# A hybrid attention and mixture-of-experts layer: the input projection in 512-column products, and the first expert pass fixed to expert 0 with its weights loaded early

## The reference, cut to what matters

```
h    = rms_norm(x);  proj = h @ w_in                      # 512 x 1024 @ 1024 x 3072
mix  = concat(diff_attention(...), silu(gate) * norm(retention(...)))
x    = x + mix @ w_o
h2   = rms_norm(x);  logits = h2 @ w_router + b_router
top_val, top_idx = top_k(logits, 4);  gates = softmax(top_val)
for every expert e, over its tokens:
    u = h2[tokens] @ w_moe_in[e] + b;  a = swiglu_clamped(u)     # 1024 -> 2048 -> 1024
    y[tokens] += gates * (a @ w_moe_out[e] + b)
out  = rms_norm(x + y)
```

## Time and profile before

| | |
|---|---|
| median of 3 executions | 1530.5 us (1530.23 to 1533.79) |
| profiled execution, its own time | 1528.76 us |
| its span | 1527.1 us |
| mean granted TensorE clock | 0.977 of full |
| PE / DVE / ACT / POOL busy | 95% / 85% / 67% / 15% of the span |
| projection on PE | about 14 to 155.4 us |
| first product of pass 0 | 334.03 us |
| DMA | 462.93 MB, mean 303 GB/s |

### The profile page before, as it was taken

How to read it: one execution, slowest core, us unless ns; L and a number is a source line. 1 busy time by engine, 2 the same in 40 slices (tenths; PEclk the granted TensorE clock), 3 DMA queues, 4 the chain that set the end, 5 groups by cost and what they waited for, 6 DMA issues and landing times.

```text
span 1527.1 us, 23128 instructions
## 1 busy us (share of the span) xinstructions
PE 1452.4 (95%) x7349; PEld 1216.0 (80%) x7349; DVE 1291.6 (85%) x1149; ACT 1024.1 (67%) x914; POOL 236.2 (15%) x239
## 2 busy tenths in 40 slices
PE   7999679849999999999999999999999999999996
PEld 7999457737888888888888888888888888888884
DVE  5643664759999999999999999999999999999997
ACT  6222562327777777777777777777777777777774
POOL 0000401230111111111111111111111111111112
PEclk9999798959999999999999999999999999999999
DMA  9420100269999999999999999999999999999994
GB/s 320 141 84 28 42 1 21 52 235 343 359 368 360 372 364 361 373 372 375 370 370 369 370 376 362 377 366 360 364 373 377 368 370 367 371 366 375 366 369 166
DMA packets 137604, 462.93 MB, mean 303 GB/s; under 512 B 15620, under 2 KB 28200, under 8 KB 137512
## 3 DMA queue, kind: packets, MB, share of 16 engines
q1 hardware_dynamic: 124000, 442.55, 77.9%
q0 software_dynamic: 13248, 19.41, 5.2%
q10 hardware_dynamic: 328, 0.60, 0.1%
HBM read 459.57 MB, written 23.36 MB: 316 GB/s over the span
## 4 chain that ended last, share of the span: by engine, by line
PE 89%; DVE 4%; DMA 3%; ACT 2%; issue 1%; SPq 0%; POOLq 0%; POOL 0%; DVEq 0%; ACTq 0%
PE pair L921 23%; PE pair L923 23%; PE pair L929 23%; PE pair L634 3%; PE pair L639 3%; PE pair L635 3%; PE pair L935 2%; PE pair L947 2%; PE pair L897 2%; DMA ring<-in_w_moe_in 2%; PE pair L788 1%; PE pair L789 1%; PE pair L799 1%; DVE split L1707 1%; DMA expert_sums<-work,list_cur 1%
## 5 line engine op out<-in xcount | busy, mean ns | idle before, releaser
L1707 DVE TENSOR_TENSOR split<-ring,split 128x2048 fp32r<-128x2048 f32 x396 | 892.9, 2287 | 72.3 <-ACT split L1212 72.3
L1212 ACT CAST split<-ring 128x2048 fp32r<-128x2048 f32 x396 | 758.7, 1916 | 214.4 <-PE pair L929 194.6
L921 PE MATMUL pair<-split,operands 128*128 128x512 f32 x1584 | 631.1, 398 | 4.6 <-DVE operands L1712 4.6
L923 PE MATMUL pair<-split,operands 128*128 128x512 f32 x1584 | 618.9, 391 | 0.0
L929 PE MATMUL pair<-split,operands 128*128 128x512 f32 x1584 | 425.2, 390 | 0.0
L921 PEld LDWEIGHTS pair<-split,operands 128*128 128x128 f32 x1584 | 298.3, 188 | 64.0 <-DVE operands L1712 5.2
L929 PEld LDWEIGHTS pair<-split,operands 128*128 128x128 f32 x1584 | 297.9, 188 | 63.4
L923 PEld LDWEIGHTS pair<-split,operands 128*128 128x128 f32 x1584 | 298.4, 188 | 58.7
L1947 POOL DMA_INDIRECT expert_sums<-work,list_cur x32 | 60.9, 1904 | 462.3 <-PE pair L929 430.8
L1940 POOL DMA_INDIRECT work<-h_rows,token_next x35 | 72.4, 2069 | 183.8 <-DMA token_next<-slot_lists 168.2
L634 PE MATMUL pair<-split,operands 128*128 128x256 f32 x352 | 86.5, 283 | 1.0 <-DVE work L1388 1.0
(11 more groups left out here) (266 smaller groups left out, 1228.1 us busy)
## 6 DMA issues: line engine op xcount, KB each, us to landing
ring<-in_w_moe_in SPq DMA_DIRECT2D x264, 1024.0 KB, 9.3
ring<-in_w_moe_out SPq DMA_DIRECT2D x132, 1024.0 KB, 10.5
ring<-in_w_in SPq DMA_DIRECT2D x12, 1024.0 KB, 10.6
ring<-in_w_o SPq DMA_DIRECT2D x4, 1024.0 KB, 4.9
resid<-in_x SPq DMA_DIRECT2D x4, 512.0 KB, 5.4
expert_sums<-zero_rows SPq DMA_DIRECT2D x4, 512.0 KB, 8.7
work<-expert_sums SPq DMA_DIRECT2D x4, 512.0 KB, 5.2
out<-ring SPq DMA_DIRECT2D x4, 512.0 KB, 2.6
```

The source lines that it names most:

```text
L921: pe.matmul(dst[:, f, :], left_hi[:, k0 + k, :], hi[c.buffer][:, k, cols], start=(start and k == 0), stop=False)
L923: pe.matmul(dst[:, f, :], left_lo[:, k0 + k, :], hi[c.buffer][:, k, cols], start=False, stop=False)
L1212: act.copy(hi[c.buffer], raw[c.slot]).then_inc(hi_made, 1)
L1707: dve.tensor_tensor(lo[c.buffer], raw[c.slot], hi[c.buffer].bitcast(F32), ALU.subtract).then_inc(lo_made, 1)
```

## The change

It has four parts. The input projection now goes in 6 blocks of `BW` = 512 columns. A chunk is half a block's K tiles (4 of 8) by 512 columns, so it still has 1 MB, and there are still 12. Two chunks accumulate into one bank; blocks alternate between banks 0 to 3 and 4 to 7, and the transposes of q and k moved to banks 0 to 3. `w_out_lo` and `w_out_hi` stand ahead of the evictions in the last two chunks. In the output projection `mix_high` isn't cut in two around `bias_product` any more. In the routing `choose` makes `picked` with one comparison over 32 x 4 and one reduction; `read_places` also makes the 0/1 matrix of places of expert 0 for its tile; the search for the first expert with tokens is gone, expert 0 always gets pass 0 (and at least one pass, even if it has no tokens); the counts and the table of passes come after the gates. And SP loads the early chunks 0, 2, 3, 4 when the last high product of the output projection is done (`wo_high_done`), 1 and 5 after the whole of it; each chunk raises its own `raw_full`. POOL issues the scatter of tile 2 after clearing `x_rows`, and the load of the last norm's gain after the scatter of tile 3.

```diff
-NCHUNK = PROJ // CW
+BW = 512
+NBLOCK = PROJ // BW
+NCHUNK = 2 * NBLOCK
...
-            def first_chunk(e, n):
-                return up_chunk(e, n // QUARTERS, n % QUARTERS)
+            def first_load(n):
+                sp.dma_start(raw[n], up_chunk(0, n // QUARTERS, n % QUARTERS)).then_inc(raw_full[n], 16)
 
             for i in range(NT - 1):
                 sp.wait_ge(h2_ready, i + 1)
                 sp.dma_start(h2_dram[i * P:(i + 1) * P, :], h2_row[:, i, :]).then_inc(h2_stored, 16)
+            sp.wait_ge(wo_high_done, 1)
+            for n in (0, 2, 3, 4):
+                first_load(n)
             sp.wait_ge(wo_done, NT)
-            sp.wait_ge(b_out_split, 1)
-            sp.wait_ge(b_in_split, 2)
-            for n in range(RAW):
-                sp.dma_start(raw[n], first_chunk(0, n)).then_inc(early_loaded, 16)
-            load_pass_count(sp)
-            first = expert_of(0)
-            sp.wait_ge(early_loaded, 16 * RAW)
-            with sp.If(first < 1):
-                for n in range(RAW):
-                    sp.sem_inc(raw_full[n], 16)
-            with sp.Else():
-                for n in range(RAW):
-                    sp.dma_start(raw[n], first_chunk(first, n)).then_inc(raw_full[n], 16)
+            for n in (1, 5):
+                first_load(n)
             sp.wait_ge(pool_passed, 1)
             for k in range(RAW - QUARTERS, QUARTERS):
-                load(0, SECOND + k, up_chunk(first, 1, k))
+                load(0, SECOND + k, up_chunk(0, 1, k))
+            load_pass_count(sp)
             by_pass(sp, one_pass)
...
             for c in range(1, NCHUNK):
+                b, a, s = c // 2, c % 2, c % PARTS
                 pe.wait_ge(w_hi_made, c + 1)
                 for i in range(NT):
-                    u = c * NT + i
-                    pe.wait_ge(proj_by_act if u % 2 == 0 else proj_by_dve, (u - 4) // 2 + 1)
-                    dst, at_i, s = bank[u % 4][:, 0:CW], of_tile(i), c % PARTS
...
+                    if a == 0 and b >= 2:
+                        pe.wait_ge(proj_by_act if i % 2 == 0 else proj_by_dve, 2 * (b - 2) + i // 2 + 1)
+                    dst, at_i = bank[NT * (b % 2) + i], of_tile(i)
+                    for k in range(KH):
+                        pe.matmul(dst, hT_hi[:, KH * a + k, at_i], w_hi[s][:, k, :], start=(a == 0 and k == 0), stop=False)
+                        pe.matmul(dst, hT_lo[:, KH * a + k, at_i], w_hi[s][:, k, :], start=False, stop=False)
                     if i == 0:
                         pe.wait_ge(w_lo_made, c + 1)
-                    for k in range(KT):
-                        mm = pe.matmul(dst, hT_hi[:, k, at_i], w_lo[s][:, k, :], start=False, stop=(k == KT - 1))
-                    mm.then_inc(proj_ready, 1)
+                    for k in range(KH):
+                        mm = pe.matmul(dst, hT_hi[:, KH * a + k, at_i], w_lo[s][:, k, :],
+                                       start=False, stop=(a == 1 and k == KH - 1))
+                    if a == 1:
+                        mm.then_inc(proj_ready, 1)
+                    elif i == NT - 1:
+                        mm.then_inc(half_block_done, 1)
...
-                    mm = pe.transpose(bank[4 + g % 4][:, i * P:(i + 1) * P], proj[:, i, col:col + P], ident)
+                    mm = pe.transpose(bank[g % 4][:, i * P:(i + 1) * P], proj[:, i, col:col + P], ident)
...
+                    if i == NT - 1 and k == KT - 1:
+                        mm.then_inc(wo_high_done, 1)
...
-                mix_high(i, range(0, 4))
+                mix_high(i, range(KT))
                 bias_product(i - 2)
-                mix_high(i, range(4, KT))
                 router(i - 1)
                 mix_low(i)
             places(2)
+            def first_tokens(j):
+                pe.wait_ge(first_list_step, j + 1)
+                for a in range(2):
+                    mm = pe.matmul(bank[2][:, 256:257], first_slots[:, j, :], token_parts_bf[:, j, a:a + 1],
+                                   start=(j == 0 and a == 0), stop=(j == NT - 1 and a == 1))
+                if j == NT - 1:
+                    mm.then_inc(first_product, 1)
+
             router(3)
+            pe.wait_ge(tokens_named, 13)
+            for j in range(NT - 1):
+                first_tokens(j)
             places(3)
-            pe.wait_ge(tokens_named, 13)
-            pe.wait_ge(first_list_step, 1)
+            first_tokens(3)
             for j in range(NT):
-                mm = pe.matmul(bank[6][:, 64:66], first_slots[:, j, :], token_parts_bf[:, j, :],
+                mm = pe.matmul(bank[3][:, 64:64 + NE], ones_bf[:, :], picked_bf[:, j, :],
                                start=(j == 0), stop=(j == NT - 1))
-            mm.then_inc(first_product, 1)
+            mm.then_inc(place_ready, 1)
...
             for c in range(NCHUNK):
-                for i in range(1, NT, 2):
...
-                    if c >= NCHUNK - 2:
-                        w_out_lo(2 * (c - NCHUNK + 2) + i // 2)
-                if c in ROPE_CHUNKS:
-                    rotary(c)
+                if c == NCHUNK - 2:
+                    for q in range(3):
+                        w_out_lo(q)
+                if c == NCHUNK - 1:
+                    w_out_lo(3)
+                if c % 2:
+                    evict(c // 2, 1)
+                if c + 2 < NCHUNK:
+                    w_in_lo(c + 2)
+                if c % 2:
+                    evict(c // 2, 3)
+                    for n in (c - 1, c):
+                        if n in ROPE_CHUNKS:
+                            rotary(n)
...
                 dve.wait_ge(place_read, i + 1)
+                dve.tensor_scalar(first_slots[:, i, :], slot_number, within[:, i, 0:1], None, ALU.is_equal)\
+                    .then_inc(first_list_step, 1)
...
-                chain(dve.tensor_copy(top8_f, top8_i))
+                chain(dve.tensor_tensor(by_choice, expert_id.unsqueeze(2).to_broadcast([P, NE, TOPK]),
+                                        top8_i[:, 0:TOPK].unsqueeze(1).to_broadcast([P, NE, TOPK]), ALU.is_equal))
                 chain.settle()
-                for k in range(TOPK):
...
-                dve.tensor_copy(picked_bf[:, i, :], picked[:, i, :]).then_inc(picked_ready, 1)
+                with nc.allow_low_precision(reason="zeros and ones"):
+                    dve.tensor_reduce(picked_bf[:, i, :], by_choice, AX_X, ALU.add).then_inc(picked_ready, 1)
+                dve.wait_ge(picked_ready, i + 1)
...
-            h2_norm(NT - 1)
             read_places(NT - 2)
             place_entries(NT - 2)
...
-            dve.tensor_copy(expert_count, bank[7][:, 64:64 + NE]).then_inc(table_ready, 1)
...
-            dve.tensor_tensor(first_slots, slot_number.unsqueeze(1).to_broadcast([P, NT, SLOTS]),
-                              first_at.unsqueeze(2).to_broadcast([P, NT, SLOTS]), ALU.is_equal).then_inc(first_list_step, 1)
-            chain(dve.tensor_scalar(n_passes, expert_count, 0.0, None, ALU.is_gt))
-            chain.settle()
             dve.wait_ge(first_product, 1)
-            chain(dve.tensor_scalar(first_at[:, 0:1], bank[6][:, 64:65], float(NOWHERE), None, ALU.add))
-            chain.settle()
-            dve.tensor_tensor(token_next[:, 0:1], bank[6][:, 65:66], first_at[:, 0:1], ALU.add).then_inc(first_list_step, 1)
+            dve.tensor_scalar(token_next[:, 0:1], bank[2][:, 256:257], float(NOWHERE), None, ALU.add)\
+                .then_inc(first_list_step, 1)
...
+            dve.wait_ge(place_ready, NT + 1)
+            dve.tensor_copy(expert_count, bank[3][:, 64:64 + NE]).then_inc(table_ready, 1)
+            dve.wait_ge(table_ready, 1)
+            chain(dve.tensor_scalar(n_passes, expert_count, 0.0, None, ALU.is_gt))
+            chain.settle()
...
-            for i in range(NT - 1):
+            for i in range(NT - 2):
                 place_entries(i)
-            pool.wait_ge(logits_ready, NT)
+            pool.wait_ge(wo_done, NT)
             pool.memset(x_rows, 0.0).then_inc(tokens_named, 1)
             pool.wait_ge(tokens_named, 14)
+            place_entries(NT - 2)
             pool.wait_ge(h2_stored, 16 * NT)
-            pool.dma_start(gf_row, for_all_partitions(norm_f_g)).then_inc(gf_loaded, 16)
...
                 gather(0)
+                pool.wait_ge(experts_listed, 5)
+                pick(0, 0)
                 place_entries(NT - 1)
+                pool.dma_start(gf_row, for_all_partitions(norm_f_g)).then_inc(gf_loaded, 16)
                 pool.wait_ge(table_ready, 2)
-                first = expert_of(0)
-                pool.wait_ge(experts_listed, 5)
-                pick(0, first)
                 load_pass_count(pool)
```

(14 more changed lines are left out.)

141 lines of the change are left out of this document (66 added, 75 removed).

## The result

The kernel after takes 1514.6 us (median of four runs, 1510.1 to 1518.3) beside 1531.2 for before on the same chip, a ratio of 0.9888 [0.9856, 0.9919]. The prediction was 1508.7, with a range of 1503 to 1514: the direction was right, the gain of some 17 us is 5 short of the 22 forecast, and the time lies just outside the range.

The account below looks back on a forecast made before the run. PE fills the pass loop, so its start counts, held by a chain of waits on early chunks and SP's branch. 8.7 (A) + 1.0 (B) + 12.1 (E) = 21.8; 1528.8 - 21.8 = 1507.0, plus 1.7: 1508.7 us, range 1503 to 1514.

Parts of the forecast that it names:

- A: Input projection on PE: fewer, wider products save 7.7 us and a dropped eviction wait 1.0, together 8.7 us less.
- B: Transposes of q and k after the projection: output weight work moved ahead of the last evictions, 1.0 us less.
- C: Output projection: all high products go first, so `bias_product(1)` no longer waits for DVE's gate copy, 0.8 us less.
- D: Routing of the last token tile on DVE: the table of passes comes 4.1 us sooner, behind C.
- E: ACT's start on pass 0: only the table holds it, 315.2 instead of 327.27, 12.1 us less with C and D inside.
- three things: Conditions of E: early chunks landed in time, the pass count's load from the table cheap, the gather in time.
- The count's load: Loading the pass count from the table before ACT starts pass 0: 0.3 us, bounds 0 and 1.0.
- gather: Rival, before pass 0: the gather of token rows, behind the h2 store, becomes the bound; up to 3.0 us more, 1511.7; chance 0.13.
- early loads: Rival, before pass 0: early chunk loads stay the bound, ACT waits for chunk 1, 3.7 us later, 1512.4; chance 0.08.
- fixed cost: Rival, input projection: fewer products save 1.4 us instead of 7.7, 6.3 more, 1515.0; chance 0.07.
- F: Pass 0, from ACT's first cast to PE's first product: no change, bounds minus 2.7 us and 0.

Follow-up runs that it names:

- proj_only: The kernel before with only the change's new input projection (half blocks of K by 512 columns): 1518.9 us, 0.9939.
- after_again: The kernel after, unchanged, run in a second session: 1511.2 us beside 1528.5 for before, 0.9880.
- rest_only: The kernel after with the old 256-column projection of before: 1521.7 us, 0.9963.
- three_held: The kernel after with only chunks 0, 2 and 1 loaded before the gather, chunks 3, 4 and 5 issued once it has landed: 1506.9 us, 0.9862.
- cast_first: The kernel after with ACT's load of the pass count moved behind its work of pass 0: 1510.7 us, 0.9887.
- lists_late: The kernel after with the eight list scatters of token tiles 1 and 2 moved behind the gather: 1524.4 us, 0.9975.
- no_lists_12: The kernel after without the eight list scatters of token tiles 1 and 2, so the lists lack these entries: 1508.6 us, 0.9869.
- chunks_late: The kernel after with all six early chunks issued in order 0 to 5 at the end of the output projection: 1510.6 us, 0.9892.
- no_lists_held: loads_first_best without the list scatters of token tiles 1 and 2, so the lists lack these entries: 1499.8 us, 0.9818.
- loads_first_best: loads_first with the chunk order of three_held and ACT's load of the pass count behind its work of pass 0: 1507.8 us, 0.9869.
- loads_first: The kernel after with POOL's four list scatters of tile 1 held until chunk 0 has landed: 1516.5 us, 0.9915.
- two_held_cast: After with chunks 0, 2 early, 1 once the h2 store landed, 3 to 5 after the gather, ACT's count load behind pass 0 work: 1507.3 us, 0.9862.
- late_three_cast: After with chunks 0 to 2 at the output projection's end, 3 to 5 after the gather, ACT's count load behind pass 0 work: 1511.0 us, 0.9869.

## Why the prediction was partly wrong

- **A, B: right.** 9.7 forecast; 10.5 in the profile, 9.3 by proj_only. The cadence of 2.72 us decided against the formula of the Trainium skill (TensorE: Matmul & The Clock Gate, Back-to-back issue gap), which would have given 1.4 for the products; the page gives it for an isolated product.
- **C: right.** The row as a whole moves by more than this, with the clock. But from the router's logits of one tile to those of the next, the stretch that holds `bias_product(1)`, it is 17.05 us in before (275.67 to 292.72), 17.07 in proj_only, and 15.94 to 16.00 in after, after_again, rest_only, three_held and cast_first: 1.1 less, 0.8 forecast.
- **D: right.** The table comes 16.6 us after the residual, before it was 21.2: 4.6 less, 4.1 forecast.
- **E: the step that failed**, as it was put: "Now nothing holds ACT but the table, if three things are there". The first was not. "Even at the old ramp of 4.6 us and the old rate the fifth, chunk 1, lands by 314.8", that is 24.7 us behind the first issue; it landed 33 us behind it (276.62 to 309.65). The old rate came from another stretch, in which scatters of tiles 2 and 3 ran too (issued from 306.7 to 320.7 in before) and did little harm; at the new place two tiles' scatters halved it. With them out of the way the step holds (lists_late, no_lists_12). The third, the gather, was priced with a store of 7.9 us; it took 15.0. D and E were to shorten the way from the residual to the first product by 11.3 us; two runs of after show 1.9 and 4.5. The count's load, 0.3 forecast with 1.0 as its bound, was 1.2 (300.57 to 301.75), with no effect, since it was off the path.
- **The rivals** "gather" (0.13) and "early loads" (0.08) both came true. I had given each a price of its own, as if independent: 27.2 and 27.9 us from the residual to the first product. It was 33.6 and 31.0. They have one cause, the low rate, and it costs more than either price. The range ended at 1514, below the 1515.0 of its own rival "fixed cost".
- **F:** 0 forecast, bounds to 2.7 less; 2.1 to 2.3 less from the first product to the end. It is the warm start that the bound had allowed for: in the first 20 us of pass 0 the granted clock was 0.86 in before and 0.96 and 0.97 in the two profiles of after. It is not safe to count on: in three_held and chunks_late it was 0.91, with 1192.8 us to the end.
- **Luck in the total.** D and E together missed by 7 to 9 us, the total by about 5. F, and in the first profile the clock before the residual, gave back what no term had counted.

What stays open is why scatters slow the loads at one time and not at another. In chunks_late tile 2's four scatters (issued from 289.2) had their packets moved from 294 to 302, beside loads at 421, 200, 320 and 410 GB/s in pieces of 2 us. That scatters slow loads and store is shown by lists_late and no_lists_12 beside after, by no_lists_held beside loads_first_best, and by the fall within loads_first; the mechanism in the DMA engines isn't shown.

three_held (1506.9) and two_held_cast (1507.3) are the fastest versions that compute everything; both are 4 us under after's second median, with intervals that still touch.

## What to carry to other kernels

A transfer that is moved earlier meets other traffic: price it with the rate of its new place, and look at GB/s, not at the DMA share alone. Two rivals that hang on the same resource are one rival, with the larger chance and both prices. Before trusting one profile of each kernel, cut the span at fixed events and see which part moves by the clock alone.

## What was not expected of the hardware

- Indirect scatters of single list entries, four of 128 per token tile, brought the chunk loads from 290 to 390 GB/s down to 67 to 160 at a DMA share near 1, and a 512 KB store from 2.8 us up to 11.7 (no_lists_held, loads_first_best), though the chunks ahead of it had hardly a packet left to move.
- Loads that started 4 to 5 us after the last scatter was issued needed another 4 to 6 us to get to their rate (before, chunks_late, late_three_cast); without scatters ahead of them they started at 244 and 279 GB/s (lists_late, no_lists_12).
- Queued in a row beside chunk loads, such scatters drain slowly: in lists_late twelve, issued from 303.8, were through at 336.7, 2.7 us each, and POOL's issue itself grew from 0.97 to up to 3.09 us.
